# One slot fewer per mixed pair: the inverse's products of a pair's second chunk share a visit with the transposes of the next pair's attention weights

## The reference

```python
h = rmsnorm(x); proj = h @ w_in
att = swa(q, k, v, sinks)          # chunks of 64, a window of two chunks
rw  = rwkv7_mix(p_rw, ...)         # a recurrence over tokens, 8 heads of 64
u   = [att, rw] @ w_branch
x   = x + (sum_b sigmoid(gate_b) * u_b) @ w_out
x   = x + (silu(h2 @ w_ffn_gate) * (h2 @ w_ffn_up)) @ w_ffn_down      # h2 = rmsnorm(x)
# the recurrence, per head and token:
S = S * w_t + (S @ -kk_t) (kk_t * a_t)^T + v_t k_t^T
o_t = S @ r_t
```

## Time and profile before

| | before |
|---|---|
| median of 3 runs | 3147.89 us (3146.59 to 3149.02) |
| the profiled execution | 3147.71 us, span 3145.9 us |
| PE busy | 3102.5 us, 99% of the span |
| DVE, ACT, POOL busy | 53%, 33%, 7% |
| granted clock of PE, mean over the span | 0.998 |

### The profile page before, as it was taken

One profiled execution on the slowest core, in us unless ns is written; L12 is line 12 of the kernel. 1 busy time (PEld: TensorE's weight loads), 2 busy tenths in 40 slices (PEclk: granted clock), 3 DMA queues, 4 the chain that ended last, 5 costly groups with the idle time before them and its releaser, 6 DMA issues.

```text
span 3145.9 us, 65881 instructions
## 1 busy us (share of the span) xinstructions
PE 3102.5 (99%) x27801; PEld 2640.2 (84%) x27801; DVE 1675.3 (53%) x2856; ACT 1035.2 (33%) x1893; POOL 223.9 (7%) x205
## 2 busy tenths in 40 slices
PE   8999999999999999999999999999999999999998
PEld 6777778888887888888888889998888889999997
DVE  6577554577777673355564275305666535532224
ACT  5545433444444443232231043303333313300001
POOL 0112100011111000011110000001111100000000
PEclk9999999999999999999999999999999999999999
DMA  4555443376666853554444673265444455455556
GB/s 162 168 191 171 157 157 99 103 248 212 211 217 216 265 185 95 179 168 146 146 142 158 193 251 96 93 217 179 133 130 130 140 161 179 153 189 177 177 177 196
DMA packets 272404, 532.28 MB, mean 169 GB/s; under 512 B 36208, under 2 KB 39664, under 8 KB 272112
## 3 DMA queue, kind: packets, MB, share of 16 engines
q1 hardware_dynamic: 272112, 528.07, 51.8%
HBM read 415.97 MB, written 112.08 MB: 168 GB/s over the span
## 4 chain that ended last, share of the span: by engine, by line
PE 93%; DVE 3%; ACT 2%; DMA 1%; issue 1%; SPq 0%; POOL 0%; DVEq 0%; ACTq 0%
PE PS L869 81%; PE PS L913 6%; PE PS L972 1%; PE PS L1038 1%; PE PS L1022 1%; PE PS L1212 1%; PE PS L962 1%; PE PS L1008 0%; PE PS L1219 0%; DMA wl<-weight_lo 0%; ACT L1237 0%; DVE wl L1677 0%; DMA raw<-w 0%; PE PS L906 0%; PE PS L998 0%
## 5 line engine op out<-in xcount | busy, mean ns | idle before, releaser
L869 PE MATMUL PS<-hh,wh 128*128 128x512 f32 x1864 | 749.5, 402 | 0.1
L869 PE MATMUL PS<-hh,wl 128*128 128x512 f32 x1864 | 727.5, 390 | 0.0
L869 PE MATMUL PS<-hl,wh 128*128 128x512 f32 x1864 | 727.2, 390 | 0.0
L1256 ACT ACTIVATE wh<-raw 128x512 fp32r<-128x512 f32 x452 | 283.4, 630 | 429.3 <-PE PS L869 354.1
L869 PEld LDWEIGHTS PS<-hh,wh 128*128 128x128 f32 x1864 | 349.9, 188 | 79.8 <-issue 2.1
L869 PEld LDWEIGHTS PS<-hh,wl 128*128 128x128 f32 x1864 | 350.0, 188 | 75.7
L1677 DVE TENSOR_TENSOR wl<-raw,wh 128x512 fp32r<-128x512 f32 x452 | 321.8, 714 | 164.3 <-ACT wh L1256 160.8
L869 PEld LDWEIGHTS PS<-hl,wh 128*128 128x128 f32 x1864 | 350.5, 188 | 67.8 <-issue 0.7
L869 PE MATMUL PS<-hh_last,wh 128*128 128x272 f32 x1280 | 266.0, 289 | 0.1
L869 PE MATMUL PS<-hl_last,wh 128*128 128x272 f32 x1280 | 264.6, 288 | 0.0
L869 PE MATMUL PS<-hh_last,wl 128*128 128x272 f32 x1280 | 263.1, 287 | 0.0
(11 more groups left out here) (306 smaller groups left out, 4667.3 us busy)
## 6 DMA issues: line engine op xcount, KB each, us to landing
wh<-weight_hi SPq DMA_DIRECT2D x500, 256.0 KB, 2.7
wl<-weight_lo SPq DMA_DIRECT2D x500, 256.0 KB, 3.0
raw<-w SPq DMA_DIRECT2D x178, 512.0 KB, 3.6
weight_hi<-wh SPq DMA_DIRECT2D x164, 256.0 KB, 4.3
weight_lo<-wl SPq DMA_DIRECT2D x164, 256.0 KB, 4.7
raw<-w SPq DMA_DIRECT2D x92, 256.0 KB, 3.1
gate_scratch<-gst SPq DMA_DIRECT2D x48, 256.0 KB, 3.7
gb<-gate_scratch SPq DMA_DIRECT2D x48, 256.0 KB, 4.4
```

The costliest lines, as they stand in the source:

```text
L869: mm = pe.matmul(PS[:, bank(t) + f, 0:t.cols], wt[:, cols], mov[:, m, (t.half + f) * t.cols:(t.half + f + 1) * t.cols], start=(first and a ...
L1256: act.activation(wh[h % 4][:], src, ACT.Copy).then_inc(hi_done, 1)
```

## The change

In the table of the mixed stretch the slot of SA1 (2.2) and the slot of PTR (2.2) become one of 3.7, and the slot of Q1 grows from 2.2 to 2.9. The width of a mixed stretch stays 19.0. The last tail of a block has no front beside it; there the old table's PTR slot is left out, so its width grows from 14.8 to 17.0 in the blocks 0 to 2, and the block's total from 184.9 to 187.1. In block 3 the total is unchanged.

```diff
-MIXED = (("SA0", "S", 2.3), ("DO0", "ZA", 2.2), (None, "KG", 2.0), ("Q1", None, 2.2), ("SA1", None, 2.2),
-         (None, "PTR", 2.2), ("DO1", "PV", 4.2), ("VAR", None, 1.7))
+MIXED = (("SA0", "S", 2.3), ("DO0", "ZA", 2.2), (None, "KG", 2.0), ("Q1", None, 2.9), ("SA1", "PTR", 3.7),
+         ("DO1", "PV", 4.2), ("VAR", None, 1.7))
```

## The result

| | before | after |
|---|---|---|
| median | 3147.6 us (7 runs, 3146.59 to 3149.02) | 3157.48 us (7 runs, 3155.13 to 3158.81) |
| ratio | | 1.0032, 95% interval 1.0022 to 1.0041 |
| the profiled execution | 3147.71 us, span 3145.9 us | 3158.81 us, span 3156.9 us |

The changed kernel is slower by 9.9 us, 0.32%. The prediction, 3146.7 us and no measurable change, was wrong, and the result lies outside its range.

The account below looks back on a forecast made before the run. It took PE's own work plus its waits as the bound (busy 3102.5 of 3145.9 us). Terms -2.7 - 7.4 - 1.1 - 0.6 + 6.9 + 1.2 + 0.8 + 1.7 = -1.2 gave 3146.7 us, range 3141.0 to 3152.0.

Parts of the forecast that it names:

- Term 1: PE's own work in the thirteen mixes: merging SA1 and PTR saves 0.21 us a visit, -2.7 us.
- a fixed part: Cost in a group of transposes counted once when merged: eight take 0.68 us instead of 0.79 alone.
- Rival 4: PE's merged visits: the merge saves no work, term 1 is zero, 3149.4 us; within the forecast's case, no separate chance.
- Term 2: PE's waits that go: block 0's `ptk`, `sm`, `sv` and half clock -7.4 us, block 1's `bkk` -1.1, `oo` -0.6.
- Term 3: Waits that come: SA1 for `rhs` in block 0 +6.9 us, DO1 +1.2, other blocks +0.8, half clock +1.7.
- the price of DVE's chain ahead of DO1: Block 0: DVE needs 5.1 us behind `rhs` against PE's 4.9; 0.4 a mix, with `bkk` +1.2 us.
- Rival 3: Blocks 1 to 3: DVE's softmax ahead of `rhs` holds up SA1 in each of ten mixes, 3154.9 us; chance 0.08.
- the shift of places: Blocks 0 to 2: visits shift by up to 2.2 units; a product step waiting for its evacuation would refute the forecast; unpriced.
- Rival 2: Block 0: the clock falls at each of the three waits for `rhs`, 3150.1 us; chance 0.12.
- Rival 1: Block 0: PE waits less than the exchange says, as DVE's scan may come sooner, 3140.4 us; chance 0.12.

Follow-up runs that it names:

- experiment 5: The changed kernel with 3, 3 and 1 matmuls of constants on PE ahead of the wait for `rhs` in block 0's mixes: 3157.49 us.
- experiment 8: Two runs: the whole change in block 0 alone, 3151.15 us; the changed kernel with LM of block 1's first pair one product step later, 3153.78 us.
- its repeat: The changed kernel with POOL's bonus products renumbered, an edit that left every engine's order as it was: 3156.86 us.
- the tail alone: The kernel before with only the last tail of each block on the new table (17.0 units instead of 14.8), nothing merged: 3151.06 us.
- LM's step: The changed kernel with one visit, LM of block 1's first pair, put one product step later, as it stood before: 3153.78 us.
- the merge alone: The kernel before with the new table in the thirteen mixes, the last tails kept old and the block's total 184.9: 3152.01 us.

## Why the prediction was wrong

**Term 1, the merged visit (-2.7): wrong in size.** A visit without a wait, in block 2:

```profile
1419.65 0.39 PE L869 MATMUL PS<-hh,wl 128*128 128x512 f32 x1
1419.97 0.68 PE L913 MATMUL PS<-rhs,pt 64*64 64x65 f32 x16
1420.58 1.09 PE L998 MATMUL PS<-mat,sm 128*128 128x128 f32 x8
...
1421.75 0.39 PE L869 MATMUL PS<-hl,wh 128*128 128x512 f32 x1
```

The transposes start 0.61 after the products, and by the prediction's own reckoning the visit takes 1421.75 - 1419.65 - 0.45 = 1.65 us against 1.69 apart; I had 1.42 to 1.53. The three merged visits of block 2, which wait for nothing, are all alike. That is 0.04 a visit, some 0.5 us in all. The step that failed is "0.68 if the other four cost what half of them cost beyond a fixed part": what I called a fixed part, from one row with four transposes, is not saved. Rival 4 was nearly right on this, but its time, 3149.4, is not the result either.

**Term 2, waits that go (-9.1 with `bkk` and `oo`): right for block 0's `ptk` and `sm`, and half right for `sv`** (0.8 stays). The wait for `bkk` stayed (1.5 in three). The 1.7 us for half clock, which I took away here and added again in term 3, was no term at all: experiment 5 shows that such stretches in the mixes of block 0 hide behind DVE.

**Term 3, SA1's waits for `rhs` (+6.9): right in size, 6.7, by errors that cancel.** `rhs` was not done when `pn` was done before, 209.23 in mix 1, but at 210.71: the scan 0.27 later, a `wl` behind it (0.6), the addition 0.76 longer beside POOL. SA1 too was later than I had it, due at 207.93 in place of 207.02, so its wait is 2.83 where I had 2.2. The other two came out shorter, 2.48 and 1.34 against 3.0 and 1.7: `rhs` was done 0.9 and 1.0 us later than I had it, and SA1 due 1.4 later, since PE already lagged. In blocks 1 to 3 the waits are 2.0 us (8.7 - 6.7) against 0.8.

**The step that failed inside term 3** is the price of DVE's chain ahead of DO1: "At 0.7 us each ... that is 4.2 + 0.9 = 5.1 us against 4.9". From the end of `rhs` to the end of `sv` the first mix takes 217.51 - 210.71 = 6.8 us. `kt` took 1.41 and `aa` 1.76 beside POOL's products, where I took the duration of the commonest operation of that size. The price is hidden in the profile: PE waits only 0.8 for `sv`, because it ran at half clock meanwhile; the fill in experiment 5 uncovers 4.0, where I had +1.2. Rival 3 had POOL in one clause, for other blocks, at 0.08. The rows were there before: `mxs<-mxs` 0.50, 0.92 and 0.56 in block 0 for an operation that takes 0.17 alone.

**What was dismissed in one sentence: the shift of places.** "The trace before shows nothing of size" of product steps waiting for an evacuation, and that was true, and no evidence: such a wait appears only when a visit crosses it. It was named as what would make the forecast wrong altogether, and it had no price and no share of the chances. Measured: 3.7 us in the changed kernel (experiment 8), 2.4 against its repeat. The same shift also brought the wait of 1.1 us for `oo` in block 1, which the tail alone has as well.

**The account.** The whole change in block 0: 3.7. LM's step: 3.7. That leaves 2.5 of 9.9 for the rest of blocks 1 to 3, where the profile has 2.0 us of new waits for `rhs` and the 1.1 for `oo`, less what merged visits save; that these are the same was not tested. Against the forecast, whose terms for block 0 add up to 1.2 (-0.6, -7.4, -0.6, +6.9, +1.2, +1.7), block 0 is off by 2.5, LM's step by 3.7, term 1 outside block 0 by 1.7, `bkk` by 1.3, and the waits for `rhs` in blocks 1 to 3 by 1.2: with `oo` 11.5 of the 11.1 us between -1.2 and +9.9, an estimate, since the terms come from different runs.

Merge and tail cost more together than apart (9.9 against 7.4). The lags say where: in block 0, at 622 us, the merge alone has 2.0, the tail alone -1.1, and both together 4.1; and at 681 us the half clock, 1.6, is in the profile of both together and not in that of the tail alone. Why block 0 loses 3.2 us more with both stays open: the rows show longer DVE chains in the one than in the other, but no run parts them. Rival 2 came true in its clock, 10.2 us at half speed in block 0 for the 3.4 of before, and is refuted as a cost. Rival 1 did not happen, and rival 3 ended on the right side by a mechanism that is small in its blocks.

## What to carry to other kernels

Sharing a visit between small matmuls saves what one row of the two back to back shows, here 0.04 us. What it costs is that the visit now waits for the later of its two inputs. Before forecasting a change of a table that scales all places, list every visit that crosses a product step, and what DVE then has ahead of the next evacuation: one such crossing cost 2.4 to 3.7 us. And take an operation's duration from the rows in which the neighbour engine works at the same time, not from the group's mean.

## What the runs showed of the hardware

POOL's operations lengthen many of DVE's with two SBUF inputs that lie beside them. The addition of 128x8 takes 0.17 us alone and 1.26 beside POOL, until POOL's operation ends; means over 16 of `kt<-aa,hka`, `aa` and `ra<-kk,zz` range from 683, 734 and 747 ns with POOL's bonus held back to 964, 899 and 779 in the kernel before and up to 1236 for `aa` with POOL's work repeated, while `rhs` (one of two inputs in PSUM) stays at 424 in all. And half clock cost about half of its stretch where the time followed PE, 1.6 us of 3.4 behind `xres` at 681 us, and next to nothing in 10.2 us of it in block 0, where DVE was the bound (3157.49 us without it, 3157.48 with it).
